# A decoder layer on one core: the output projection taken by halves, the experts' lists in pairs, row additions that skip unrouted places, and half of each expert's second product in split parts

## The chip, the cores and the metric

The kernel runs on one core of a Trainium2 chip. The metric is the device time of one execution in microseconds, the median of several runs. All data is float32.

## The reference, cut to what matters

```python
for i in range(DEPTH):                      # DEPTH = 1, SEQ = 512 tokens, D_MODEL = 1024
    ...                                     # S5 branch and windowed attention give `merged`
    x = x + merged @ w_out[i]               # 512x1024 @ 1024x1024
    h2 = rmsnorm(x, norm_ffn[i])
    x = x + hierarchical_moe(h2, ...)

def hierarchical_moe(h, w_coarse, w_fine, w_up, w_down):
    coarse = softmax(t @ w_coarse)          # 4 groups, the best one is taken
    fine = (t @ w_fine)                     # 16 experts, the best 2 in that group
    ...
    act = silu(g_part) * u_part * gates     # w_up: 1024 -> 2 x 256 for each expert
    out = einsum('nef,efd->nd', act, w_down)  # w_down: 256 -> 1024
```

So 512 tokens with two experts each make 1024 (token, expert) pairs, over 16 experts.

## The kernel before, in words

A float32 product on TensorE costs several passes. The kernel therefore splits most operands into a high and a low part of type fp32r (ScalarE copies the high part, VectorE or GpSimd subtracts it from the raw value), and takes three products of the parts (`product`). The experts' second product and the router take plain float32.

The output projection (`P_OUT`, `NOUT` = 4 weight pieces of 256 columns) goes over `TT` = 4 tiles of 128 tokens. Tile 0 goes piece by piece, the other three take two pieces (512 columns) at once. `x2` is the residual stream. For each tile `norm2` multiplies x2 by the gain into `xg`, ScalarE squares x2 to get the variance, GpSimd takes the inverse root, TensorE transposes xg (`turn_norm2`), VectorE copies it out (`norm2_turned`), `router` multiplies it with the router's weights. These steps of tile t-1 stand between the products of tile t, those of the last tile behind everything.

Then VectorE works out the routing (some 40 small dependent instructions). A list of 128 places is made for each expert: `pos` gives each token a place, first the tokens that are routed to the expert, then the others in order; `pick` compares it with the place numbers, and four matmuls (`place_list`) with `tg` (columns: token number, the gate's high and low part, the token number again) give `idx_all` and `gate_all`. Unrouted tokens have gate 0. The lists of experts 0 to 7 are made before the first expert, those of 8 to 15 at once in step 3.

Step e of the expert loop, in the order of each engine's own queue:

- TensorE: `up(e)` (24 matmuls of 512 columns), in step 3 the lists, `turn_act(e-1)` (2 transposes), `turn_rows(e+1)` (8 transposes), `down_(e-1)` (4 float32 matmuls of 512 columns).
- ScalarE: `high_up(e+1,0)`, `rows_out(e-2)` (PSUM times gate into `y_out`), `high_up(e+1,1)`, `turned_act(e-1)`, a tanh, `high_rows(e+1)`. It waits for the load of expert e+1 at the head of this queue.
- VectorE: in step 3 the lists, `low_up(e+1)` in two halves, `low_rows(e+1)`, `swiglu(e)`.
- GpSimd: `add_rows(e-5)` adds the 128 rows of an expert to the output in memory; it waits until the addition before it has landed. Then it gathers the rows of expert e.
- SyncE loads the weights: 2 MB for `up` into a ring of five places, 1 MB for `down` into four. The first four ring places are those of the output projection's pieces, free when `piece_used` says so; the fifth is x2's. Later, `up` of expert e+5 waits for up(e), and behind it the `down` of e+4 waits for down(e), both in the one queue.

Of the kernel before, what the change touches and what calls it, by code (L numbers as in the profile page):

```python
# [6 lines left out]
F32 = mybir.dt.float32  # L7
# [7 lines left out]
P = 128  # L15
# [9 lines left out]
def hybrid_layer(nc, x, norm_mix, w_in, lam_re, lam_im, log_dt, b_re, b_im, c_re, c_im, d_skip,  # L25
# [26 lines left out]
    LISTS = [0, 2, NE // 2, NE]  # L52
# [7 lines left out]
    with ExitStack() as ctx:  # L60
# [98 lines left out]
        xgT = [part("raw", 2 * D + D * i, D, k=DC, n=P) for i in range(2)]  # L159

# [4 lines left out]
        actT = [part("att", 1280 + 2 * D + 256 * i, 256, k=2, n=P) for i in range(2)]  # L165
        th_e = [part("ssm", 4 * DOWN + 256 * i, 256) for i in range(2)]
# [22 lines left out]
        ssq = sb("ssq", [P, 2 * TT])  # L189
# [25 lines left out]
        idx_all = sb("idx_all", [P, NE], U32)  # L215
        gate_all = sb("gate_all", [P, NE])
# [63 lines left out]
        gather_turn = sem("gather_turn")  # L280

# [58 lines left out]
        def piece_used(eng, n):  # L340
# [35 lines left out]
        def split_low(eng, n):  # L376
# [5 lines left out]
                              ).then_inc(low_done_p if n in on_pool else low_done_v, 1)  # L382

# [30 lines left out]
        def _(sp):  # L414
# [29 lines left out]
            sp.dma_start(sink[:], sinks[0:1, :].broadcast_to([P, HEADS])).then_inc(small_loaded, 16)  # L444
            sp.dma_start(rw[:, :, 0:NG], w_coarse[0].rearrange("(k p) n -> p k n", p=P)).then_inc(small_loaded, 16)
# [54 lines left out]
        def _(g):  # L500
# [137 lines left out]
        def _(act):  # L638
# [169 lines left out]
            for t in range(TT):  # L808
                act.wait_ge(x2_done, NOUT * (t + 1))
                act.activation(part("att", t % 2 * D, D), x2[:, t, :], ACT.Square, accum_out=ssq[:, TT + t:TT + t + 1]).then_inc(sq_done, 1)  # L810
# [3 lines left out]
                act.wait_ge(n2_done, t + 1)  # L814
# [21 lines left out]
            def turned_act(e):  # L836

                act.wait_ge(at_full, e + 1)
                act.activation(actT[e % 2], sc[1][:, 0:2 * P].rearrange("p (k n) -> p k n", k=2), ACT.Copy).then_inc(at_done, 1)  # L839
# [35 lines left out]
            rows_out(NE - 2)  # L875
            turned_act(NE - 1)
# [19 lines left out]
        def _(v):  # L896
# [19 lines left out]
            def norm2(t):  # L916

                if t == 0:
# [3 lines left out]
                if t >= 2:  # L922

                    v.wait_ge(h2_scaled, t - 1)
                    v.wait_ge(tp_full, n_tp + 2 * (t - 1))
                v.wait_ge(x2_done, NOUT * (t + 1))
                tt(xg[t % 2], x2[:, t, :], ffn_gain, ALU.mult).then_inc(n2_done, 1)
                v.wait_ge(sq_done, TT + t + 1)
                mean_var(ssq[:, TT + t:TT + t + 1], D)

            def norm2_turned(t):
                if t >= 2:
                    v.wait_ge(lg_full, t - 1)
                for f in range(2):
                    v.wait_ge(tp_full, n_tp + 2 * t + f + 1)
                    v.tensor_copy(xgT[t % 2][:, 4 * f:4 * f + 4, :], tp[f][:].rearrange("p (k n) -> p k n", k=4)
                                  ).then_inc(h2T_done, 1)
# [63 lines left out]
            v.wait_ge(small_loaded, 16 * 14)  # L1001
# [271 lines left out]

            v.wait_ge(gates_done, 2 * DC)
# [17 lines left out]
            for t in range(TT):  # L1292
                if t:
                    norm2(t - 1)
                for p_ in range(NOUT):
                    n = NOUT * t + p_
                    if t == 0 and p_ + 1 < NOUT:
                        split_low(v, P_OUT + p_ + 1)
                    xs = x2[:, t, p_ * 256:(p_ + 1) * 256]
                    if t == 0:  # L1300
                        v.wait_ge(pj_full, n_pj + n + 1)
                        got = pj[n % 2][:, 0:256]
                    else:
                        v.wait_ge(pj_full, n_pj + NOUT * t + p_ // 2 * 2 + 2)
                        got = pj[p_ // 2][:, (1 - p_ % 2) * 256:(2 - p_ % 2) * 256]
                    stt(xs, got, 0.5, xs, ALU.mult, ALU.add).then_inc(x2_done, 1)
                    if t and p_ == NOUT // 2 - 1:
                        norm2_turned(t - 1)
            norm2(TT - 1)
            norm2_turned(TT - 1)  # L1310

            v.wait_ge(const_ready, 10)
            for n in (0, 3):
                mark(v.tensor_copy(tg[:, :, :, n], bc(tok_id[:, :].rearrange("p (o t) -> p o t", o=1), [P, NE, TT])))
            mark(v.memset(rt[:, 7, 0:1, :], 0.0))
            v.wait_ge(lg_full, TT)
# [53 lines left out]
            v.wait_ge(lg_full, TT + 1)  # L1370
            link(v.tensor_copy(r(10), sc[0][:, 0:TT * NE].rearrange("p (t e) -> p t e", t=TT)))
            mark(ts(r(7), r(6), -1.0, 1.0, ALU.mult, ALU.add))
            v.wait_ge(lg_full, TT + 2)
# [8 lines left out]

# [489 lines left out]
```

## Time and profile before

| | us |
|---|---|
| runs, median (lowest, highest) | 625.59 (621.91, 627.24) |
| the profiled execution's own time | 628.41 |
| its span in the trace | 626.7 |
| mean granted TensorE clock, share of full | 0.931 |
| TensorE busy | 551.8 |
| VectorE busy | 375.3 |
| ScalarE busy | 262.8 |

A busy TensorE is one with a matmul in flight; matmuls overlap, so a row's duration is longer than the step from one start to the next. The chain of waits is the chain of work that ended last, followed back from the last instruction.

### The profile page before, as it was taken

The numbers are of one execution on the slowest core, as the hardware profiler recorded it, in microseconds if no ns is written. First come the engines' busy times: TensorE is split into PE (matmuls) and PEld (weight loads), VectorE is DVE, ScalarE is ACT, GpSimd is POOL, SyncE is SP. The second block draws the span as 40 slices with busy tenths as digits, with TensorE's granted clock in tenths as the row PEclk, the third lists the DMA queues.
The fourth block names the chain that finished last, engine by engine and source line by source line (L and its number), as shares of the span: only waits on it lengthen the run. The fifth ranks groups of instructions, "written<-read, shape, count | busy, mean of one in ns | idle before, by whom it ended". The sixth has DMA issues, their size and how long they took to land.

```text
span 626.7 us, 7175 instructions
## 1 busy us (share of the span) xinstructions
PE 551.8 (88%) x2589; PEld 432.6 (69%) x2589; DVE 375.3 (60%) x615; ACT 262.8 (42%) x421; POOL 191.5 (31%) x354
## 2 busy tenths in 40 slices
PE   1699799999979899989999789935799999999982
PEld 1488687887667677677888678835668677676750
DVE  3885176683983884956666632365865766665530
ACT  6415035435433545364223311131463666665631
POOL 2549333089469269000000000002021341313111
PEclk9999799988989989999999889965897999999997
DMA  8524520220220210113364561597479799999954
GB/s 302 107 69 110 160 66 2 68 67 2 68 67 2 67 51 1 52 51 100 98 208 158 208 253 68 200 396 276 126 262 347 243 376 340 372 341 371 345 96 69
DMA packets 69220, 102.82 MB, mean 164 GB/s; under 512 B 10528, under 2 KB 42304, under 8 KB 69184
## 3 DMA queue, kind: packets, MB, share of 16 engines
q1 hardware_dynamic: 63184, 80.84, 37.6%
q0 software_dynamic: 4608, 16.78, 10.7%
q10 hardware_dynamic: 1392, 4.74, 1.9%
q8 instruction: 21, 0.34, 0.2%
q14 instruction: 15, 0.12, 0.1%
HBM read 88.71 MB, written 12.58 MB: 162 GB/s over the span
## 4 chain that ended last, share of the span: by engine, by line
PE 61%; DVE 15%; DMA 7%; ACT 7%; POOL 4%; issue 3%; SPq 1%; ACTq 0%; POOLq 0%; DVEq 0%
PE pj L1477 8%; PE pj L1479 8%; PE pj L1478 8%; PE m L1794 7%; DMA arena_front<-in_w_expert_up_dram 4%; PE pj L1774 4%; PE pj L1775 4%; PE pj L1776 4%; PE sc L1554 2%; PE tp L1762 2%; ACT arena_back L755 1%; SPq L481 1%; DMA arena_front<-h_rows,idx_all 1%; DVE arena_back L1190 1%; ACT arena_back L764 1%
## 5 line engine op out<-in xcount | busy, mean ns | idle before, releaser
L1477 PE MATMUL pj<-h_high,split 128*128 128x512 f32 x192 | 81.3, 424 | 2.7 <-DVE h_low L963 1.5
L1478 PE MATMUL pj<-h_low,split 128*128 128x512 f32 x192 | 78.4, 409 | 0.0
L1479 PE MATMUL pj<-h_high,split 128*128 128x512 f32 x192 | 78.2, 407 | 0.0
L1411 DVE TENSOR_TENSOR up_low<-arena_front,up_high 128x2048 fp32r<-128x2048 f32 x26 | 59.2, 2290 | 21.9 <-ACT up_high L827 21.9
L1794 PE MATMUL m<-arena_back 128*128 128x512 f32 x128 | 58.3, 598 | 2.8 <-ACT arena_back L839 2.8
L605 POOL DMA_INDIRECT out_dram<-arena_back,idx_all x16 | 29.8, 1866 | 101.2 <-DMA out_dram<-arena_back,idx_all 87.4
L1774 PE MATMUL pj<-up_high,xt_high 128*128 128x512 f32 x128 | 56.1, 438 | 5.3 <-DVE up_low L1411 3.7
L519 POOL TENSOR_TENSOR rstd<-ssq,half_col 128x1 f32<-128x1 f32 x8 | 6.4, 796 | 166.2 <-DVE ssq L940 166.2
L827 ACT ACTIVATE up_high<-arena_front 128x2048 fp32r<-128x2048 f32 x26 | 49.5, 1916 | 6.6 <-DMA arena_front<-in_w_expert_up_dram 5.7
L1775 PE MATMUL pj<-up_low,xt_high 128*128 128x512 f32 x128 | 50.7, 396 | 0.0
L1776 PE MATMUL pj<-up_high,xt_low 128*128 128x512 f32 x128 | 50.7, 396 | 0.0
L1477 PEld LDWEIGHTS pj<-h_high,split 128*128 128x128 f32 x192 | 38.7, 202 | 15.6 <-issue 6.0
L381 POOL TENSOR_TENSOR split<-arena_front,split 128x2048 fp32r<-128x2048 f32 x8 | 36.4, 4551 | 41.3 <-ACT split L374 40.7
L374 ACT ACTIVATE split<-arena_front 128x2048 fp32r<-128x2048 f32 (+1 forms) x23 | 40.4, 1760 | 16.0 <-PE sc L1479 10.0
L1479 PEld LDWEIGHTS pj<-h_high,split 128*128 128x128 f32 x192 | 38.2, 199 | 8.7
L1478 PEld LDWEIGHTS pj<-h_low,split 128*128 128x128 f32 x192 | 38.7, 201 | 7.6
L1794 PEld LDWEIGHTS m<-arena_back 128*128 128x128 f32 x128 | 23.3, 192 | 26.8 <-issue 23.2
L596 POOL DMA_INDIRECT arena_front<-h_rows,idx_all x16 | 18.4, 1151 | 62.1 <-PE tp L1762 40.1
L1477 PE MATMUL pj<-split,m_high 128*128 128x512 f32 (+1 forms) x80 | 30.0, 375 | 6.6 <-DVE split L381 2.8
L381 DVE TENSOR_TENSOR split<-arena_front,split 128x1536 fp32r<-128x1536 f32 (+1 forms) x15 | 30.1, 2004 | 9.6 <-ACT split L374 8.6
L1774 PEld LDWEIGHTS pj<-up_high,xt_high 128*128 128x128 f32 x128 | 24.6, 192 | 14.6 <-issue 6.9
L1406 DVE TENSOR_TENSOR xt_low<-tp,xt_high 128x512 fp32r<-128x512 f32 x32 | 20.7, 685 | 21.7 <-ACT xt_high L833 21.7
(316 smaller groups left out, 1241.4 us busy)
## 6 DMA issues: line engine op xcount, KB each, us to landing
arena_front<-in_w_expert_up_dram SPq DMA_DIRECT2D x13, 2048.0 KB, 15.9
arena_back<-in_w_expert_down_dram SPq DMA_DIRECT2D x16, 1024.0 KB, 12.8
arena_front<-in_w_in_dram SPq DMA_DIRECT2D x13, 1024.0 KB, 5.6
arena_back<-in_w_expert_up_dram SPq DMA_DIRECT2D x3, 2048.0 KB, 17.3
arena_front<-in_w_out_dram SPq DMA_DIRECT2D x4, 1024.0 KB, 5.3
arena_back<-in_x_dram SPq DMA_DIRECT2D x4, 512.0 KB, 5.9
arena_front<-in_w_ssm_glu_gate_dram SPq DMA_DIRECT2D x8, 256.0 KB, 2.8
arena_front<-in_w_ssm_glu_val_dram SPq DMA_DIRECT2D x8, 256.0 KB, 3.6
```

What stands on the lines that cost most here:

```text
L374: nc.scalar.activation(w_high[split_place(n)][:, 0:z], raw[n % 2][:, 0:z], ACT.Copy).then_inc(high_done, 1)
L381: eng.tensor_tensor(w_low[s][:, 0:z], raw[n % 2][:, 0:z], w_high[s][:, 0:z].bitcast(F32), ALU.subtract).then_inc(low_done_p if n in on_poo ...
L605: g.indirect_dma_start(out_rows, bass.IndirectOffsetOnAxis(idx_all[:, e:e + 1], 0), y_out[e % 2], None, compute_op=ALU.add).then_inc(y_add ...
L827: act.activation(up_high[e % 2][:, half(h)], ring[e % NU][:, half(h)], ACT.Copy).then_inc(up_high_done, 1)
L1411: tt(up_low[e % NU][:, half(h)], ring[e % NU][:, half(h)], up_high[e % 2][:, half(h)].bitcast(F32), ALU.subtract).then_inc(up_low_done, 1)
L1477: pe.matmul(dst, sh, mh, start=first and i == 0, stop=False)
L1478: pe.matmul(dst, sh, ml, start=False, stop=False)
L1479: ins = pe.matmul(dst, sl, mh, start=False, stop=last and i == len(terms) - 1)
L1774: pe.matmul(pj[e % 2][:], xs[0], ws[0], start=k == 0, stop=False)
L1775: pe.matmul(pj[e % 2][:], xs[0], ws[1], start=False, stop=False)
L1776: ins = pe.matmul(pj[e % 2][:], xs[1], ws[0], start=False, stop=k == DC - 1)
L1794: ins = pe.matmul(mb[h][:], actT[e % 2][:, k, :], down[e % 4][:, k, h * 512:(h + 1) * 512], start=k == 0, stop=k == 1)
```

## The change

1. The output projection goes over 8 units, `UNITS`: first the left 512 columns of all four tiles, then the right ones. Units 0 and 7 go by pieces of 256 columns, the others in one. In the middle of each unit's products stand the 4 transposes of the unit before, and behind them its half of the router (4 of the 8 terms). TensorE now transposes x2 itself, and the gain is multiplied into the router's weights `rw` once, early; a load `gain_col` (1024 numbers, one each to a partition and column) is added to SyncE's queue at the start. The squares are summed by halves. `piece_used` lets pieces 0 and 1 go after unit 3.
2. The lists of experts 8 to 15 are made in pairs, in steps 1 to 4, and read a step later.
3. `tg`'s fourth column gets token number + 512 for unrouted tokens. It is read into `idx_own`, which the additions use with a bounds check, so that a place with an unrouted token is passed over. The gathers still fetch all 128 rows.
4. The first of the two k-parts of each expert's second product goes in split parts: `high_down` (ScalarE, 128x1024), `low_down` (VectorE, 128x1024), `turned_act` as two copies of 128 columns, `low_act` (VectorE, 128x128); TensorE has two float32 matmuls and six in fp32r where it had four in float32.

```diff
-    LISTS = [0, 2, NE // 2, NE]
+    LISTS = [0, 2] + list(range(NE // 2, NE + 1, 2))
@@ piece_used
-                eng.wait_ge(pj_full, n_pj + NOUT * (TT - 1) + (n - P_OUT) // 2 * 2 + 2)
+                eng.wait_ge(pj_full, n_pj + 2 * TT * ((n - P_OUT) // 2 + 1))
+        UNITS = [(hf, t) for hf in range(2) for t in range(TT)]
+        BY_PIECE = (0, len(UNITS) - 1)
+        LAST_LISTS = len(LISTS) - 3
@@ sync
+            sp.dma_start(gain_col[:], norm_ffn[0].rearrange("(k p) -> p k", p=P)).then_inc(small_loaded, 16)
@@ gpsimd
-                g.indirect_dma_start(out_rows, bass.IndirectOffsetOnAxis(idx_all[:, e:e + 1], 0), y_out[e % 2], None,
-                                     compute_op=ALU.add).then_inc(y_added, 16)
+                g.indirect_dma_start(out_rows, bass.IndirectOffsetOnAxis(idx_own[:, e:e + 1], 0), y_out[e % 2], None,
+                                     compute_op=ALU.add, bounds_check=SEQ - 1, oob_is_err=False).then_inc(y_added, 16)
@@ scalar
+                act.activation(actT[e % 2][:, 1, :], sc[1][:, P:2 * P], ACT.Copy).then_inc(at_done, 1)
+                act.activation(at_high[e % 2][:], sc[1][:, 0:P], ACT.Copy).then_inc(at_done, 1)
+            def high_down(e):
+                act.wait_ge(down_loaded[e % 4], 16 * (e // 4 + 1))
+                act.activation(dn_high[:], down[e % 4][:, 0, :], ACT.Copy).then_inc(dn_high_done, 1)
@@ step(e): behind rows_out(e - 2)
+                if e >= 1:
+                    high_down(e - 1)
@@ vector, output projection
+            for u in range(2, 2 * TT - 1):
+                hf, t = UNITS[u]
+                if hf:
+                    gained(0, t)
+                for i in range(2):
+                    row_piece(u, i)
+                if hf:
+                    gained(1, t)
+                    variance2(t)
+                turned2(u)
+            gained(0, TT - 1)
+            last = 2 * TT - 1
+            row_piece(last, 0)
+            turned2_piece(last, 0)
+            row_piece(last, 1)
+            gained(1, TT - 1)
+            turned2_piece(last, 1)
+            variance2(TT - 1)
@@ vector, expert loop
             for e in range(NE):
-                if e == 3:
-                    fill_lists(2)
+                if 1 <= e <= LAST_LISTS:
+                    for n in range(LISTS[e + 1], LISTS[e + 2]):
+                        pick_list(n)
+                if 2 <= e <= LAST_LISTS + 1:
+                    read_lists(e)
                 if e + 1 < NE:
                     low_up(e + 1, 0)
+                if e:
+                    low_down(e - 1)
+                if e + 1 < NE:
                     low_up(e + 1, 1)
+                if e:
+                    low_act(e - 1)
+                if e + 1 < NE:
                     low_rows(e + 1)
                 swiglu(e)
@@ tensor, output projection
+            for u in range(1, 2 * TT - 1):
+                ...
+                out_pair(u, first_k)
+                for i in range(2):
+                    turn_rows2(u - 1, i)
+                out_pair(u, last_k).then_inc(pj_full, 2)
+                router(u - 1)
+            ...
+            out_piece(u, 0, first_k)
+            for i in range(2):
+                turn_rows2(u - 1, i)
+            out_piece(u, 0, last_k).then_inc(pj_full, 1)
+            router(u - 1)
+            out_piece(u, 1, first_k)
+            turn_rows2(u, 0)
+            out_piece(u, 1, last_k).then_inc(pj_full, 1)
+            turn_rows2(u, 1)
+            router(u)
@@ down_(e)
                 for h in range(2):
-                    for k in range(2):
-                        ins = pe.matmul(mb[h][:], actT[e % 2][:, k, :], down[e % 4][:, k, h * 512:(h + 1) * 512], start=k == 0, stop=k == 1)
+                    pe.matmul(mb[h][:], actT[e % 2][:, 1, :], down[e % 4][:, 1, cols[h]], start=True, stop=False)
+                pe.wait_ge(dn_low_done, e + 1)
+                pe.wait_ge(at_low_done, e + 1)
+                for h in range(2):
+                    pe.matmul(mb[h][:], at_high[e % 2][:], dn_high[:, cols[h]], start=False, stop=False)
+                    pe.matmul(mb[h][:], at_high[e % 2][:], dn_low[e % 4][:, cols[h]], start=False, stop=False)
+                    ins = pe.matmul(mb[h][:], at_low[e % 2][:], dn_high[:, cols[h]], start=False, stop=True)
                 ins.then_inc(dn_full, 1)
```

## Rows read from the trace of the kernel before

**Rows 1.** Windows: us, busy time (instructions) of each engine, granted clock, DMA share, GB/s

```profile
360.30:362.20 1.90, 0.00 (x0) 0.00 (x0) 1.90 (x2) 0.00 (x0) 0.00 (x0) 1.00 1.03 414
362.20:367.60 5.40, 5.33 (x28) 5.23 (x29) 0.86 (x3) 0.23 (x1) 0.00 (x0) 0.68 0.99 392
488.80:594.40 105.60, 105.60 (x445) 75.15 (x446) 67.77 (x63) 66.40 (x83) 29.22 (x19) 1.00 1.04 350
```

**Rows 2.** Chain of waits (start, us, what), output projection to first gather

```profile
378.67 1.69 PE sc L1701 x16
...
385.97 0.87 PE tp L1695 x8
...
405.98 0.77 DVE arena_back L1306 x2
406.87 1.24 DVE arena_front L927
...
410.25 3.42 PE sc L1701 x16
413.69 0.69 DVE arena_back L1319 x4
...
428.02 7.14 DMA arena_front<-h_rows,idx_all
```

**Rows 3.** DMA issues in the window 435:448: form, count, median us to landing

```profile
arena_front<-h_rows,idx_all POOLq DMA_INDIRECT x1, 4.4
```

**Rows 4.** Timeline of TensorE (start, us, line, operation): lists, a middle expert

```profile
476.39 0.95 PE L1753 MATMUL sc<-tg,pick 128*128 128x4 f32 x8
...
543.61 0.39 PE L1774 MATMUL pj<-up_high,xt_high 128*128 128x512 f32 x1
...
544.29 0.38 PE L1784 MATMUL sc<-ident,arena_back 128*128 128x128 f32 x2
```

**Rows 5.** Chain of waits, second products of four steps

```profile
467.63 3.44 PE m L1794 x8
...
484.99 3.80 PE m L1794 x8
...
525.51 3.44 PE m L1794 x8
535.53 3.44 PE m L1794 x8
```

**Rows 6.** Timeline of VectorE, a middle step (idle before it in brackets)

```profile
552.18 2.29 DVE L1411 TENSOR_TENSOR up_low<-arena_front,up_high 128x2048 fp32r<-128x2048 f32 x1 [1.72 <-ACT up_high L827]
```

**Rows 7.** Timeline of ScalarE, the same step

```profile
554.73 0.38 ACT L839 ACTIVATE arena_back<-sc 128x256 f32<-128x256 f32 x1 [2.58 <-PE sc L1784]
```

**Rows 8.** Timeline of SyncE's queue: loads for the experts' first products

```profile
399.64 10.31 SPq L467 DMA_DIRECT2D arena_front<-in_w_expert_up_dram  x4
...
448.38 0.37 SPq L467 DMA_DIRECT2D arena_front<-in_w_expert_up_dram  x1
...
489.23 0.47 SPq L467 DMA_DIRECT2D arena_front<-in_w_expert_up_dram  x1
```

**Rows 9.** Chain of waits, the last load and the end

```profile
566.51 24.80 DMA arena_front<-in_w_expert_up_dram
...
596.53 3.70 PE m L1794 x8
...
610.21 1.27 ACT arena_back L848 x2
...
611.75 6.26 DMA out_dram<-arena_back,idx_all
```

**Rows 10.** Timeline of GpSimd, two additions

```profile
544.46 1.59 POOL L605 DMA_INDIRECT out_dram<-arena_back,idx_all  x1 [7.28 <-DMA out_dram<-arena_back,idx_all]
...
618.76 1.55 POOL L605 DMA_INDIRECT out_dram<-arena_back,idx_all  x1 [5.46 <-DMA out_dram<-arena_back,idx_all]
```

**Rows 11.** DMA queues in the window 611.5:626.7: packets, MB, share of 16 engines

```profile
q0 software_dynamic: 288, 1.05, 44.8%
```

More of the change, by code:

```diff
@@ L159, in hybrid_layer @@
         xgT = [part("raw", 2 * D + D * i, D, k=DC, n=P) for i in range(2)]
+        x2T = [part("rot", 512 * i, 512, k=4, n=P) for i in range(2)]
         xt_high = [rounded("xt_high0", "raw", 2 * D, [P, DC, P]), rounded("xt_high1", "u4", 0, [P, DC, P])]
@@ L165, in hybrid_layer @@
         actT = [part("att", 1280 + 2 * D + 256 * i, 256, k=2, n=P) for i in range(2)]
+        at_high = [rounded(f"at_high{i}", "att", 1280 + 2 * D + 256 * i, [P, P]) for i in range(2)]
+        at_low = [rounded(f"at_low{i}", "att", 1792 + 2 * D + P * i, [P, P]) for i in range(2)]
+        dn_high = rounded("dn_high", "att", 0, [P, D])
+        dn_low = [rounded(f"dn_low{s}", "ssm", s * DOWN, [P, D]) for s in range(4)]
         th_e = [part("ssm", 4 * DOWN + 256 * i, 256) for i in range(2)]
@@ L280, in hybrid_layer @@
         gather_turn = sem("gather_turn")
+        dn_high_done, dn_low_done, at_low_done = (sem(n) for n in ("dn_high_done", "dn_low_done", "at_low_done"))
         pj_order, tp_order = [], []
@@ L875, in _ @@
             rows_out(NE - 2)
+            high_down(NE - 1)
             turned_act(NE - 1)
@@ L1419, in swiglu, with low_down, low_act @@
                 stt(act_e[b], a1_e[b], 0.5, pj[b][:, DE:UP_N], ALU.mult, ALU.mult).then_inc(act_done, 1)
+            def low_down(e):
+                v.wait_ge(dn_high_done, e + 1)
+                tt(dn_low[e % 4][:], down[e % 4][:, 0, :], dn_high[:].bitcast(F32), ALU.subtract).then_inc(dn_low_done, 1)
+            def low_act(e):
+                v.wait_ge(at_done, 2 * (e + 1))
+                tt(at_low[e % 2][:], sc[1][:, 0:P], at_high[e % 2][:].bitcast(F32), ALU.subtract).then_inc(at_low_done, 1)
             low_rows(0)
@@ L1732, in _, with turn_rows2 @@
-            turn_norm2(TT - 1)
-            router(TT - 1)
+            def turn_rows2(u, i):
+                hf, t = UNITS[u]
+                pe.wait_ge(x2_done, 2 * u + i + 1)
+                if u < 2:
+                    pe.wait_ge(tp_free[u], (n_tp + 1 - u) // 2)
+                else:
+                    pe.wait_ge(h2T_done, 2 * u if u == BY_PIECE[1] and i else 2 * (u - 1))
+                for k in range(2):
+                    c0 = hf * 512 + (2 * i + k) * P
+                    ins = pe.transpose(turned_bank(u, i)[:, k * P:(k + 1) * P], x2[:, t, c0:c0 + P], ident[:])
+                ins.then_inc(tp_full, 1)
@@ new lines, in router, with out_piece @@
+            def router(u):
+                hf, t = UNITS[u]
+                for k in range(4):
+                    if k % 2 == 0:
+                        pe.wait_ge(h2T_done, 2 * u + k // 2 + 1)
+                    ins = pe.matmul(sc[0][:, t * (NG + NE):(t + 1) * (NG + NE)], x2T[u % 2][:, k, :], rw[:, 4 * hf + k, :],
+                                    start=u == 0 and k == 0, stop=hf == 1 and k == 3, skip_group_check=True)
+                ins.then_inc(lg_full, 1)
+            def out_piece(u, i, ks):
+                hf, t = UNITS[u]
+                w = piece_w(P_OUT + 2 * hf + i, k=DC, n=256)
+                tok = slice(t * P, (t + 1) * P)
+                for k in ks:
+                    if u == 0 and i == 0:
+                        pe.wait_ge(m_low_done, k + 1)
+                    ins = product(out_bank(u, i), [(both(m_hl, k, tok), both(w, k, slice(None)))], k == 0, k == DC - 1)
+                return ins
@@ new lines, in out_pair @@
+            def out_pair(u, ks):
+                hf, t = UNITS[u]
+                tok = slice(t * P, (t + 1) * P)
+                w2 = [x[:, hf].rearrange("p s (k n) -> p s k n", k=DC) for x in (out_high, out_low)]
+                return product(pj[(u + 1) % 2][:].rearrange("p (s n) -> p s n", s=2),
+                               [(both(m_hl, k, tok), both(w2, slice(None), k, slice(None))) for k in ks], ks[0] == 0, ks[-1] == DC - 1)
+            first_k, last_k = range(DC // 2), range(DC // 2, DC)
@@ L1735, in _ @@
+            u = 2 * TT - 1
+            pe.wait_ge(x2_done, 2 * (u - 1))
+            out_piece(u, 0, first_k)
+            for i in range(2):
+                turn_rows2(u - 1, i)
[6 more added lines that the diff above has]
+            router(u)
             pe.wait_ge(r_pe, 1)
```

198 lines of the change are left out of this document (96 added, 102 removed).

## The prediction

> **What bounds the kernel now.** I read the windows first. From 488.8 to 594.4 us TensorE is busy without a gap at the full clock, and the DMA share is 1.04: both are full, and a change that helps one of them alone soon meets the other [rows 1]. In the output projection there is a hole of 1.9 us and behind it 5.4 us at a mean clock of 0.68 [rows 1]. The chain of waits says where the path runs: TensorE to 405.98, then a serial stretch of VectorE, transposes, a router at 3.42 us instead of 1.69, the routing, and the first gather (7.14 us, landed at 435.2) [rows 2]. At the end it leaves TensorE: it passes through a weight load of 24.8 us (issued at 566.51, landed at 591.31), two second products, an addition to memory and the last addition [rows 9]. TensorE's own steps are 525.51 to 535.53, 10.02 us each [rows 5]; 535.53 to 596.53 is 61.0 us for six steps, 0.9 more than six times 10.02, so the late load costs about 0.9 us now [rows 5, 9].
>
> **Output projection.** Matmuls are the same: 96 of 256 columns, 144 of 512. The hole at 360.3 (1.9 us) is tile 0 waiting for the fourth weight piece [rows 1]. By halves the pieces 2 and 3 are wanted only at unit 4, behind three units of some 6.8 us, so the hole goes, and with it the slow clock behind it: 0.32 of 5.4 us, 1.7 us [rows 1]. Together 3.6. The earlier stalls (fp32r parts of m, piece 1) stay. Against it, more transposes and router work now stand ahead of the last product: before it were 3 x 0.87 and 2 x 1.69 = 6.0 us [rows 2]; after it are 7.5 halves of the transposes (3.3) and 7 halves of the router (5.9), 9.2 us. The last product ends 0.4 us earlier.
>
> Behind it stood 405.98 to 413.69, 7.7 us: additions, gain product 1.24, transposes, copies, router 3.42 [rows 2]. Now: addition of one piece 0.4 (half of 0.77), two transposes 0.3, a gain product of half width 0.6, a copy 0.4, four of the router's instructions 0.4 to 0.9, and 0.1 for each handover, 2.6 to 3.0 us. The variance (a square of half width, VectorE, GpSimd's root) runs beside it and should end at about the same time. That saves 4.9. In the routing itself `tg`'s new column adds one dependent instruction and two small copies, 0.4 us by the sizes around it (0.69 for four) [rows 2]. So the first gather is asked for 4.9 us earlier.
>
> Two of the four first loads go at about 377 instead of 399.64 [rows 8], when the DMA has little to do. They are 4 MB of the 10 MB that stood ahead of and beside the first gather. That gather took 7.14 us from its issue, one with the queue free 4.4 [rows 2, 3]: between 0 and 2.7 saved; I take 2.7, since the last of the loads should now be down by 422. The loads themselves gain nothing more: all five places were full before up(0) ended anyway, and load 5 waits for it. Sum up to up(0): 7.6 us earlier. The added load and the scaling of `rw` stand in stretches where VectorE waits for other loads; by the sizes of their neighbours 0 to 0.5 us if that cover is gone, 0 taken.
>
> **Lists.** From 467.63 to 484.99 one step takes 17.36 us, and its second product 3.80 for 3.44: 7.7 us over a plain one [rows 5]. TensorE and VectorE take turns there, and the clock falls. In pairs, VectorE makes both `pick`s before TensorE needs them, and TensorE pays 8 matmuls, 0.95 us [rows 4], in four steps: 3.8. Saved 3.9. If the picks aren't hidden, two of 0.69 more in each step; the cover is VectorE's idle time, about 3.6 us a step (105.6 us hold 67.8 busy, ten and a half steps) [rows 1].
>
> **Second product.** Eight float32 records take 3.44 us, 0.86 for a matmul of 512 columns [rows 5]; three fp32r products take 544.29 - 543.61 = 0.68 [rows 4]. Two of four are exchanged: 2 x 0.18 = 0.36 us for each expert, 5.4 over the 15 ahead of the last. This is the time on TensorE; the rest must be hidden. ScalarE gets 1.2 us more (1.27 for two of 512 columns [rows 9]) and 0.2 for a second copy, of an idle 2.58 [rows 7]. VectorE gets 1.24 (as the gain product [rows 2]) and 0.3; before, it ended low_up at 552.18 + 2.29 = 554.47, with 1.72 idle ahead of it, and up ended at 544.29 + 10.02 = 554.31 [rows 4, 6]. Following the queues, in a step of 9.65 us low_act is done about 1.4 us after up ends, and TensorE wants it at 2.8 (transposes 1.1, two float32 products 1.7): covered by 1.4, and by 0.9 in the steps with lists. So 0 for that; next would be low_act.
>
> TensorE alone would thus come to 7.6 + 3.9 + 5.4 + 0.9 (the late load gone) = 17.8 us earlier at its last second product.
>
> **The loads.** This is the step on which the size depends. A faster TensorE asks for loads sooner, but the DMA was full from the load issued at 489.23 to the landing at 591.31: 102.1 us [rows 1, 8, 9]. That load came 40.85 us after the one behind up(0) [rows 8]. Now it comes 40.85 - 7.7 + 3 x 0.95 - 3 x 0.36 = 34.9 us after. If the work of the queue is the same, the last weights land 137.0 us after up(0) instead of 142.9: with the 7.6 us, 13.5 us earlier than before, against some 17 that TensorE could use. ScalarE waits for this load at the head of its queue, with high_down now behind it as well (1.1 later), and two cheaper second products give back 0.7. The second product of the last expert would come 13.1 us earlier.
>
> Does the passing over relieve the queue? Of 2048 places 1024 are routed, so half of the rows go. An addition with the queue free takes 44.8% of 15.2 us / 2 = 3.4 us of all 16 engines [rows 11], so the most that it can give is 1.7 for each of the 12 additions in the full stretch, 20 us, far more than the 4 that are missing. The least is nothing. The reason for nothing is in how the rows are dealt out: the two additions have 288 packets, 2 x (128 + 16), so every one of 16 engines has eight rows and one packet more [rows 11]. Routed tokens stand first in the list; an addition and a load are done when their slowest engine is. If an engine's rows are a block of places, the engines of the first half of the list keep all eight, and only the others are relieved. If the rows are dealt in turn, all are relieved. No row of before decides it. I take no relief, because the packets show a fixed share to each engine, and keep the other end for the range.
>
> The Trainium skill, page "DMA: Bandwidth & Descriptors", section "The descriptor swizzle", says that a 128-partition transfer is dealt by partition, engines 0 to 7 serving partitions 0 to 63. By that rule about the first 64 places keep their engines as busy as before and the additions become no shorter: the first of the two results below. No row here shows which engine took which row.
>
> **The sum.** Without relief the last two additions are as before: 611.75 + 6.26, then 618.76 to the end [rows 9, 10]. -13.1 against the profiled 628.41 (its span is 626.7, 1.7 less) gives 615.3; the median of the runs lies 2.8 below that execution, so 612.5. I say 612.
>
> **Rivals.**
> *The additions relieve all engines.* For it: half of the rows are gone; against it the fixed shares. Then TensorE is the bound to the end, -17.8. The end itself shortens: each of the last two additions takes 1.7 us less, half of the 3.4 [rows 11]; but the last second product comes about 1 us later behind high_down, so that the last addition finds its rows ready only 0.6 us sooner: -2.3. Together -20.1, median 605.5.
> *The new work isn't covered.* VectorE's chain (low_up, low_down, low_up, low_act) is longer than I followed it and TensorE waits in each step. It decides from 1.4 us a step. At 0.4 us over that, 15 x 0.4 = 6 takes the gain of the split away; with the loads then just in time, median 613 to 621, say 617.
> *The check makes the additions slow to issue.* An issue takes 1.59 us, and an addition starts when the one before has landed, every 10.0 us in the middle (7.28 of that waiting) [rows 10]. With two result buffers rows_out, and with it TensorE, waits once this chain falls about 5 us further behind. If going through 128 indices with a check costs 2 us more each time, the chain goes at 12.0: 15 x 2.0 - 5 = 25 us later than the steps of 10.0, beside 12 earlier at the front: median about 638. It decides from about 1.3 us more per issue. Against it: 1.59 us for 128 rows is 12 ns for a row, and a comparison is little beside building the row's descriptor.
> *The change doesn't pass over anything* (all rows still go): the same as the forecast.
>
> **How the numbers follow.** Forecast (no relief, or none in effect) 0.47, with its own range 607 to 617: 2.7 for the gather, 2 for the end of the loads to either side. Full relief 0.32 (601 to 608). New work not covered 0.13. Slow additions 0.06; other 0.02. About 1%, 6.3 us, is what a measurement of this kernel can tell from no change; faster by more is below 619.3. Forecast and relief lie below it wholly, of the third case two thirds: 0.47 + 0.32 + 0.08 = 0.87; within 1% 0.07; slower 0.06. The range 601 to 618 leaves out most of the last two cases' far sides.
>
> **What would show it.** The hole at 360 is gone and the router's last part ends near 408; the first gather starts near 423 and takes under 5 us; steps 1 to 4 take 10.6 us each, later ones 9.65, with second products of 3.1; the lists' step of 17 us is gone. The forecast is right if the DMA share stays at 1.04 from 480 on, the last load takes over 25 us to land and TensorE waits 3 to 5 us in the last steps, and if an addition at the end still takes 6.3 us. The relief shows in a share below 1 in the middle and an addition of about 4. I am wrong if low_act or dn_low ends TensorE's waits in the middle, or if GpSimd's issues grow beyond 3 us.

## The result, and the profile after

The changed kernel takes 620.83 us, the median of 20 runs (616.33 to 625.73), against 626.04 for 20 runs of the kernel before (621.91 to 632.18). The ratio is 0.9909, with a 95% interval of 0.9887 to 0.9932, so some 4 to 7 us faster. 612 was predicted, with a range of 601 to 618. Its profiled execution took 618.26 us (span 616.5, mean clock 0.944).

The two profiled executions differ by 10.2 us, more than the medians do. Not all of that belongs to the change: the first matmul of the projection's second weight piece, which lies ahead of all that the change reorders, starts at 353.00 us before and at 350.06 after. It stands anywhere from 347.5 to 355.0 in kernels that are the same up to there. So 2.9 us of the 10.2 are scatter, and I compare the traces from fixed places on. From that first matmul to the end of the span it is 273.7 us before and 266.4 after, 7.3 less. From the first row of the routing (413.69 before [rows 2], 405.27 after) to the end it is 213.0 and 211.2, only 1.8 less. The experiments differ behind the routing only, and are compared from its first row too.

The chain of waits of the kernel after (start, us, what):

```profile
398.98 0.80 PE sc L1806 x8
...
405.27 0.69 DVE arena_back L1390 x4
...
419.97 7.84 DMA arena_front<-h_rows,idx_all
...
472.65 1.72 PE m L1916 x4
...
483.17 1.72 PE m L1916 x4
...
501.61 0.87 PE tp L1883 x8
...
511.23 0.87 PE tp L1883 x8
...
555.17 24.35 DMA arena_front<-in_w_expert_up_dram
579.57 1.80 issue
581.36 1.25 ACT arena_back L890 x2
582.61 0.95 ACT dn_high L881
583.55 1.81 ACT up_high L863
...
601.58 3.31 PE m L1916 x4
...
609.07 1.25 POOL out_dram L636
```

The front end did what it should: the routing starts 8.4 us earlier than in [rows 2]. The steps with lists take 10.52 us (472.65 to 483.17), the later ones 9.62 to 9.64 (501.61 to 511.23), where it was 17.36 and 10.02 [rows 5]. But the gather takes 7.84 us where 4.4 was counted on (7.14 before; in the experiments that leave its surroundings as they are it takes 7.2 to 8.1). At the end the chain runs through the last load as it did [rows 9], and behind it dn_high now stands ahead of up_high.

Windows of the same kernel (us, busy time of PE, PEld, DVE, ACT, POOL, granted clock, DMA share, GB/s):

```profile
362.20:367.60 5.40, 5.40 (x31) 4.51 (x29) 2.18 (x3) 0.00 (x0) 0.00 (x0) 1.00 0.42 167
...
390.00:404.00 14.00, 13.48 (x99) 12.44 (x97) 6.02 (x12) 3.59 (x6) 0.83 (x2) 1.00 0.39 154
404.00:419.10 15.10, 4.18 (x21) 3.81 (x20) 11.55 (x58) 5.33 (x7) 0.55 (x1) 0.62 0.97 349
419.10:427.80 8.70, 5.47 (x24) 5.34 (x24) 4.42 (x11) 0.00 (x0) 2.81 (x2) 0.50 0.97 349
...
500.00:560.00 60.00, 59.60 (x274) 45.77 (x273) 46.56 (x47) 43.33 (x61) 19.30 (x12) 1.00 0.98 342
544.30:579.50 35.20, 31.69 (x141) 23.34 (x140) 23.60 (x24) 22.17 (x30) 10.62 (x7) 1.00 0.96 325
579.50:606.70 27.20, 22.78 (x85) 15.08 (x83) 11.63 (x14) 12.87 (x21) 6.33 (x3) 0.94 0.30 57
```

The stretch that had a granted clock of 0.68 [rows 1] has 1.00. While the gather is under way the DMA share is 0.97. In the last two stretches TensorE is idle for 3.5 and 4.4 us. Most of that is time behind late loads; the last two waits, 0.37 and 2.31 us, are not, since e1 below has both of them although its loads are in time. ScalarE waits for the loads at the head of its queue (waits from 340 us on: us, times, longest):

```profile
POOL out_dram L636 <- DMA out_dram<-arena_back,idx_own: 91.6, 14, 8.6
...
ACT up_high L863 <- DMA arena_front<-in_w_expert_up_dram: 12.6, 4, 4.4
```

SyncE's queue: the first four loads go in two pairs; then the fifth, the one behind up(0), and the last of these loads:

```profile
374.18 0.99 SPq L498 DMA_DIRECT2D arena_front<-in_w_expert_up_dram  x2
...
402.98 0.99 SPq L498 DMA_DIRECT2D arena_front<-in_w_expert_up_dram  x2
416.57 0.37 SPq L498 DMA_DIRECT2D arena_back<-in_w_expert_up_dram  x1
...
441.49 0.37 SPq L498 DMA_DIRECT2D arena_front<-in_w_expert_up_dram  x1
...
555.17 4.25 SPq L498 DMA_DIRECT2D arena_front<-in_w_expert_up_dram  x1
```

And TensorE's timeline at the last expert's second product:

```profile
601.58 3.31 PE L1916 MATMUL m<-arena_back 128*128 128x512 f32 x4 [2.31 <-ACT arena_back L875]
603.90 1.42 PE L1920 MATMUL m<-dn_high,at_high 128*128 128x512 f32 x1
```

The last addition alone (window 608.5 to 616.5). The first line is the busy share of the 16 DMA engines in 40 equal slices, in tenths; then packets, MB, share of 16 engines, and its issue with us to landing:

```profile
DMA  0000000000019047023635636556200000000000
...
q0 software_dynamic: 144, 0.27, 23.4%
...
out_dram<-arena_back,idx_own POOLq DMA_INDIRECT x1, 6.2
```

GpSimd's timeline gives what it waited for:

```profile
608.77 1.55 POOL L636 DMA_INDIRECT out_dram<-arena_back,idx_own  x1 [5.87 <-ACT arena_back L890]
```

It moves about half of the bytes (65 of 128 rows) and keeps the engines busy for 23.4% of 8.0 us = 1.87 us, where 44.8% of 15.2 / 2 = 3.4 us were used [rows 11]. It lands in 6.2 us nevertheless; the last but one of before took 6.26 [rows 9].

### The profile page after: what moved, and what is told of

It is laid out like the page before. It is cut to its first block, busy times and chain, and to the rows that moved or that the text cites. A ratio compares the mean times of both kernels' runs of the same rounds, so it can differ in the third digit from the quotient of the medians.

```text
span 616.5 us, 7391 instructions
## 1 busy us (share of the span) xinstructions
PE 540.5 (88%) x2621; PEld 431.0 (70%) x2621; DVE 400.0 (65%) x665; ACT 279.2 (45%) x461; POOL 196.6 (32%) x354
## 4 chain that ended last, share of the span: by engine, by line
PE 58%; DVE 15%; DMA 10%; ACT 8%; POOL 4%; issue 3%; SPq 1%; ACTq 0%; POOLq 0%; DVEq 0%
PE pj L1578 9%; PE pj L1580 8%; PE pj L1579 8%; DMA arena_front<-in_w_expert_up_dram 8%; PE pj L1895 3%; PE m L1916 3%; PE pj L1896 3%; PE pj L1897 3%; PE sc L1655 2%; PE tp L1883 1%; DMA arena_front<-h_rows,idx_all 1%; ACT arena_back L786 1%; DVE arena_back L1253 1%; ACT arena_back L795 1%; DVE up_low L1493 1%
## 5 line engine op out<-in xcount | busy, mean ns | idle before, releaser
L636 POOL DMA_INDIRECT out_dram<-arena_back,idx_own x16 | 33.3, 2079 | 101.6 <-DMA out_dram<-arena_back,idx_own 91.6
L1895 PE MATMUL pj<-up_high,xt_high 128*128 128x512 f32 x128 | 51.1, 399 | 5.3 <-DVE up_low L1493 3.7
L1916 PE MATMUL m<-arena_back 128*128 128x512 f32 x64 | 31.9, 624 | 6.1 <-ACT arena_back L875 6.1
L627 POOL DMA_INDIRECT arena_front<-h_rows,idx_all x16 | 20.2, 1260 | 50.1 <-PE tp L1883 32.2
L1580 PE MATMUL pj<-split,m_low 128*128 128x512 f32 (+1 forms) x80 | 28.4, 355 | 0.0
L1897 PEld LDWEIGHTS pj<-up_high,xt_low 128*128 128x128 f32 x128 | 24.6, 192 | 5.4
```

The lines of the kernel that those rows point to most:

```text
L1580: ins = pe.matmul(dst, sl, mh, start=False, stop=last and i == len(terms) - 1)
L1895: pe.matmul(pj[e % 2][:], xs[0], ws[0], start=k == 0, stop=False)
L1897: ins = pe.matmul(pj[e % 2][:], xs[1], ws[0], start=False, stop=k == DC - 1)
L1916: pe.matmul(mb[h][:], actT[e % 2][:, 1, :], down[e % 4][:, 1, cols[h]], start=True, stop=False)
```

## The experiments

Each is the changed kernel with the edit shown. "From the routing" is the span of its profiled execution from the routing's first row to the end: 211.2 us for the changed kernel. Ratios are to the kernel before, timed with each group of experiments on the same chip; from the routing, each figure is one execution.

### What the passing over gives, and to whom

Theory: the additions move half of the bytes, but the DMA engines that serve the first half of the places stay as busy as before, so neither the additions nor the loads beside them end sooner. Rival: the loads are not the bound, and something else eats the gain.

`e1_spread`: the order of the places in `slot_no`, so that each group of four partitions holds either low places or high ones, and partitions 0 to 31 and 64 to 95 have the low ones.

```diff
-            g.iota(slot_no[:], pattern=[[1, CAP]], ...
+            g.iota(slot_no[:], pattern=[[8, 2], [64, 2], [1, 8], [16, 4]], ...
```

> The changed kernel with the place numbers of a list permuted, so that routed tokens (the first ones in the list) are laid over all 16 engines if the engine is 8 x (place / 64) + (place / 4 mod 8). Theory A (the additions relieve only the engines that hold the second half of the places): now all engines are relieved, the last addition falls from 6.2 us to about 4.5, the load that landed at 579.5 comes 5 us or more earlier, TensorE's waits in the last four steps (about 1 to 2 us each) go, and the time falls by 6 to 10 us. Theory B (a row that is passed over costs as much as one that is moved, or the flight is latency): no change, within 1 us. Theory C (the late load only uncovers the new order of the queues; the load itself is late for lack of total DMA time): the share is the same on average, so at most 2 us.

Measured: 611.12 us, ratio 0.9756 (0.9704 to 0.9807); 202.5 from the routing, 8.7 less. The waits of ScalarE for loads are gone, and all but one of GpSimd's for landed additions too (from 400 us on):

```profile
POOL out_dram L636 <- ACT arena_back L890: 72.4, 15, 8.1
...
POOL out_dram L636 <- DMA out_dram<-arena_back,idx_own: 4.4, 1, 4.4
```

Its last addition alone (window 602.6 to 609.6) lands in 5.2 us, where about 4.5 was expected:

```profile
DMA  0000000000000990261199958311000000000000
...
q0 software_dynamic: 144, 0.27, 31.3%
...
out_dram<-arena_back,idx_own POOLq DMA_INDIRECT x1, 5.2
```

`e2_block`: another order, in which each block of eight partitions has four low places and four high ones.

```diff
+            g.iota(slot_no[:], pattern=[[1, 16], [16, 8]], ...
```

> The same idea for the other way of dealing: places permuted so that routed tokens are laid over all engines if the engine is place / 8. 
Measured: 620.05 us, ratio 0.9895 (0.9834 to 0.9955), 211.6 from the routing: as the changed kernel. So the order doesn't help by being mixed; it has to be mixed in the right way. Its last addition (window 613 to 621.7) lands in 6.3 us:

```profile
DMA  0000000000000924903076452654210000000000
```

`e3_noskip`: the additions take `idx_all` without a bounds check, as before.

> The changed kernel with all 128 rows of each list added (the list with true token numbers for all places, no bounds check), the rest as changed. Theory A: the engines of the first places are as busy as in the changed kernel, so the time is the same within 1.5 us. If the passing over does relieve the loads already: slower by 3 us or more, with the last loads landing later.

Measured: 620.68 us, ratio 0.9904 (0.9873 to 0.9936). As placed in the change, passing over unrouted rows is worth nothing that the runs can tell (213.3 from the routing, 2.1 more, in one execution each).

`e12_spread_noskip`: the order of e1, and the additions of e3.

> Spread places, but the additions pass over nothing: every one of 128 rows is added, as in the kernel before. If the gain of the spread places (1.5% of the time before) comes from the passing over being dealt evenly to the 16 engines, it goes here: the ratio returns to that of the changed kernel, 0.990, with the last addition at 6.2 us. If the order of the places helps by itself (gathers and additions touching other rows at a time), it stays at 0.976.

Measured: 619.41 us, ratio 0.9892 (0.9843 to 0.994), 210.8 from the routing. The gain of e1 is gone. Its last addition (window 607.5 to 615.5), and its waits (from 400 us on):

```profile
DMA  0000000000099392766899999997200000000000
...
POOL out_dram L636 <- DMA out_dram<-arena_back,idx_all: 96.3, 15, 8.4
```

The four kernels form a square. In the old order passing over leaves the ratio where it was (0.9904 without, 0.9909 with it); in the new one it takes off 0.0136 (0.9892 and 0.9756), 8.5 us. The order brings nothing without the passing over. So the gain is the relief, evenly dealt. The packets show the dealing. Behind the first short peak, which all four have, the busy share of the last addition is at most 0.7 in the changed kernel and in e2; in e1 and e12 it reaches 0.9. Counted from the traces' DMA records, 8 packets of 4 KB are under way at a time for 1.90 us in the changed kernel (never more than 11), in e2 for 1.93 us (never more than 11). In e1 it is 16 for 1.20 us, and 16 for 1.71 us in e12, up to 20 in both. So with rows passed over, about half of the engines do all the work in the changed kernel and in e2, and all of them share it in e1.

The page "DMA: Bandwidth & Descriptors" of the Trainium skill, section "The descriptor swizzle", gives each engine, in a transfer to 128 partitions, two groups of four partitions, 32 apart, engines 0 to 7 the first 64 partitions. By that rule the changed kernel and e2 leave eight engines with all their rows and e1 leaves every engine with about half; the three runs and the counts of packets agree. Which engine took which row is not seen in the traces.

### What the split second product is worth

`e4_nosplit`: four float32 matmuls again, without `high_down`, `low_down`, `low_act`. `e8_spread_nosplit`: the same on top of e1.

```diff
-            high_down(e - 1) ... low_down(e - 1) ... low_act(e - 1)
-                    pe.matmul(mb[h][:], at_high[e % 2][:], dn_high[:, cols[h]], ...)   # and dn_low, at_low
+                    for k in range(2):
+                        ins = pe.matmul(mb[h][:], actT[e % 2][:, k, :], down[e % 4][:, k, cols[h]], ...)
```

> The changed kernel with the experts' second product wholly in float32, as before (no high_down, low_down, low_act). Theory A (the end is set by the loads): the middle steps take 10.0 us instead of 9.64 but the last load lands at nearly the same distance, high_down is not behind it and the last product isn't split: the same time or up to 2 us faster. Rival (TensorE's time counts): slower by 15 x 0.36 = 5.4 us.

> The spread lists with the second product wholly in float32. With the unspread lists this was about 2 us faster than the split one. If the loads were the bound there and TensorE is the bound now, it is slower than the spread lists with the split by 15 x 0.36 = 5.4 us less what the plain end gives back (2 to 2.5): 3 us slower, steps of 10.0 us against 9.64. Rival (the split itself isn't worth anything): the same or faster.

Measured: e4 618.32 us, ratio 0.9886 (0.9837 to 0.9934), 209.1 from the routing; e8 615.69 us, 0.9835 (0.9779 to 0.9892), 206.1. While the loads bind, the split brings nothing and perhaps costs 1 to 2 us (0.9909 against 0.9886, the intervals overlap). Once they don't, it saves 3.6 us from the routing (3 was expected) and 0.0079 of the time, 4.9 us, the intervals overlapping a little; 5.4 were predicted for TensorE. In e4, steps take 10.02 us instead of 9.64, and the last load still lands 173.8 us behind the routing's first row, against 174.3: TensorE's pace did not set it.

### The first gather

`e5_hold`: e1, and the fifth load waits until the first gather has landed. `e11_hold_alone`: the same without e1's order.

```diff
             sp.wait_ge(x2_stored, 16 * TT)
+            sp.wait_ge(gathered[0], 16)
             load_up(4)
```

> The spread lists and one thing more: SyncE asks for the fifth weight load only when the first gather has landed. In the changed kernel that gather took 7.8 us, with the load issued at 416.57 and the gather at 419.97, where a lone gather takes 4.4. If the fifth load is what the gather shares the DMA with, it takes about 4.5 us now and everything behind it comes 3 us earlier (ratio 0.005 lower than with spread lists alone). Rival: the gather is slow for another reason (its rows were stored only shortly before, or the second gather runs beside it), and it stays above 7 us; or the later load is missed in step 3 and costs as much.

> The changed kernel with its own order of places, and the fourth weight load held until the first gather has landed. It tells whether time gained at the first gather reaches the end while the loads bind. If the last weights land at a fixed distance behind the load that follows the first expert's products, the 3 us gained at the gather come through whole: 3 us less from the projection's second piece to the end. If the queue has a fixed amount of work from 489 us on and is simply full, the last load lands when it did, and nothing or at most 1 us is gained.

Measured: e5 608.99 us, ratio 0.9743 (0.969 to 0.9796), 199.8 from the routing, 2.7 less than e1. The ratio is only 0.0013 lower (0.005 was expected), 0.8 us, less than the runs can tell. Its first gather lands in 4.7 us (window 420 to 427, in which a second is issued whose landing the trace lacks):

```profile
arena_front<-h_rows,idx_all POOLq DMA_INDIRECT x2, 4.7
```

up(0) starts 25.4 us behind the routing's first row instead of 28.5. So the fifth load is what stretched the gather (e11's first gather also takes 4.7 us, with the old order of places); what stands next is TensorE, which has 24 matmuls of the second lists ahead of the transposes.

e11: 617.94 us, ratio 0.9852 (0.9796 to 0.9908), 210.3 from the routing, 1.0 less than the changed kernel. Here up(0) is 2.9 us sooner (25.4 instead of 28.3), the load behind it 2.3 (33.9 instead of 36.2), but the last load lands only 0.9 sooner (173.4 instead of 174.3). By this one execution two thirds of a gain at the front are lost in the full queue. The medians (a ratio 0.0057 lower, 3.6 us) allow the whole of it, with overlapping intervals, so this stays open. (The expectations of e11 and e9 call this load the fourth; it is `load_up(4)`, the fifth.)

### Smaller edits

`e7_gather`: e1, and the gathers pass over unrouted places too.

```diff
-                                     bass.IndirectOffsetOnAxis(idx_all[:, e:e + 1], 0)).then_inc(gathered[e % 2], 16)
+                                     bass.IndirectOffsetOnAxis(idx_own[:, e:e + 1], 0),
+                                     bounds_check=SEQ - 1, oob_is_err=False).then_inc(gathered[e % 2], 16)
```

> The spread lists, and the gathers pass over unrouted places too (rows of unrouted places keep what the buffer held; their gate is 0). If the first gather is slow by its own bytes, it falls from 7.8 to 5 to 6 us and the time by 2 us. If it is slow by the loads beside it, by half of that or less. In the middle nothing should change, since with spread lists TensorE no longer waits for loads: within 1 us.

Measured: 609.16 us, ratio 0.974 (0.9691 to 0.979); 201.9 from the routing, 0.6 less than e1, too little to tell. The first gather takes 7.02 us there and 8.08 in e1, where 5 to 6 was expected if its own bytes set it.

`e6_lastplain`: e1, with the last expert's second product in plain float32 and without `high_down(15)`, `low_down(15)`, `low_act(15)`.

> The spread lists, and the last expert's second product in float32 as before (15 of 16 in split parts). In the changed kernel TensorE waited 2.3 us for it behind high_down, and its first four records ran at half the clock (3.31 us instead of 1.98). If that is the cost of the split at the end, the gap is 1.5 us, the product 3.7 us instead of 5.1, and the end comes 2 to 2.5 us earlier. Rival: the last addition waits for the addition before it, so that half or more of this is lost.

Measured: 609.26 us, ratio 0.9732 (0.9684 to 0.9781); 200.8 from the routing, 1.7 less than e1 (2 to 2.5 was expected). TensorE's last second product:

```profile
596.29 3.70 PE L1919 MATMUL m<-arena_back 128*128 128x512 f32 x8 [1.47 <-ACT arena_back L877]
```

It waits 1.47 us instead of 2.31, and its 3.70 us compare with 5.05 (601.58 to 606.63) for the split one of the changed kernel. The granted clock is 1.00 over the 3.70 us and 0.66 over the 5.05.

`e10_order`: the changed kernel with one move in VectorE's queue.

```diff
                 if e:
                     low_down(e - 1)
+                    low_act(e - 1)
                 if e + 1 < NE:
                     low_up(e + 1, 1)
-                if e:
-                    low_act(e - 1)
```

> The changed kernel with one thing changed: on VectorE low_act(e - 1) stands ahead of low_up(e + 1, 1), which waits for ScalarE's copy of a load. Theory: in the last steps, where the loads come late, TensorE's second part of a second product waits for at_low only because low_act is queued behind the low part of a late load; with it ahead, the four waits of TensorE on at_low (1.8 us in all) go, and the time falls by 1 to 2 us. Rival: low_act moved forward waits itself for at_high, up to 3 us in each step, and pushes low_up(e + 1, 1) and so the up products later; then the steps in the middle grow beyond 9.64 us and the time rises by up to 10 us.

Measured: 623.18 us, ratio 0.9924 (0.989 to 0.9958); 215.4 from the routing, 4.1 more. My theory fell: nothing was gained. Of the rival, the longer steps are shown; that the whole becomes slower is not, since the ratio is only 0.0015 above the changed kernel's and the intervals overlap. VectorE's timeline of a middle step:

```profile
507.52 0.29 DVE L1509 TENSOR_TENSOR at_low<-sc,at_high 128x128 fp32r<-128x128 f32 x1 [2.42 <-ACT at_high L876]
507.73 2.28 DVE L1493 TENSOR_TENSOR up_low<-arena_front,up_high 128x2048 fp32r<-128x2048 f32 x1
509.92 1.28 DVE L1488 TENSOR_TENSOR xt_low<-tp,xt_high 128x512 fp32r<-128x512 f32 x2
```

VectorE waits 2.42 us with low_up queued behind it, and TensorE's next first product waits for xt_low. The chain of waits shows up_low every 10.2 us, where a step took 9.6:

```profile
497.58 2.20 DVE up_low L1493
...
507.81 2.19 DVE up_low L1493
...
518.02 2.20 DVE up_low L1493
```

`e9_all`: the edits of e1, e5, e6 and e7 together.

> The version with spread places, the fourth weight load held behind the first gather, the gathers passing over unrouted places, and the last expert's second product in plain float32, all four together. Each of the last three was run on top of the spread places and took 4.1, 0.7 and 3.1 us off the stretch from the projection's second piece to the end in its one profiled execution, but only 0.1 to 0.3% off the ratio of the medians. If the profiled savings are real and add up, this comes 7 to 8 us below the version with spread places alone: ratio to the kernel before 0.963 to 0.966. If they are mostly scatter between executions, it stays at the ratio that each of them had, 0.971 to 0.975.

Measured: 607.48 us, ratio 0.9674 (0.9627 to 0.972), the best of all and faster than both kernels; 198.5 from the routing, 3.9 less than e1. The ratio is 0.0082 lower than e1's, 5.1 us. The 4.1, 0.7 and 3.1 us in the expectation were taken from the projection's second piece and had scatter between it and the routing in them: from the routing they are 2.7, 0.6 and 1.7, together 4.9, so 3.9 to 5.1 is nearly the sum. The ratio itself lies between the two ranges that were expected (0.963 to 0.966 and 0.971 to 0.975), and its interval reaches into both. A window of it, where TensorE has no gap and the queue moves more than in the changed kernel (342 GB/s):

```profile
500.00:560.00 60.00, 60.00 (x275) 46.45 (x275) 49.60 (x50) 47.17 (x62) 17.31 (x13) 1.00 1.05 378
```

## Why the prediction was wrong

The direction was right, and so was the choice that the additions give no relief and the loads set the end; but two steps failed, the first gather and the end behind the last load, and the fall came out at less than half of the forecast (5.2 us between the medians, where the sum had 13.1). The forecast took 13.1 us off the profiled execution. From the projection's second piece on, 7.3 came off. By its steps:

| step | predicted | measured |
|---|---|---|
| routing's first row | -5.3 | -5.5 (60.69 to 55.21 behind the second piece) |
| routing to the gather's issue | +0.4 | +0.4 (14.33 to 14.70) |
| gather and up(0), to the load behind up(0) | -2.7 | +1.2 |
| that load to the landing of the last one | -5.9 | -4.9 (142.9 to 138.0) |
| landing to the end of the last second product | +0.4 | +2.9 (24.2 to 27.1) |
| from there to the end | 0 | -1.3 (11.2 to 9.9) |
| sum (before rounding) | -13.1 | -7.3 |

*Output projection: right.* The hole and the low clock behind it went, the serial stretch became short, and the gather is asked for 5.1 us earlier (4.9 predicted).

*The gather: the step that failed most.* I wrote that the last of the loads "should now be down by 422". I had followed the first four and not the fifth. It waits until the residual rows are stored, and is issued at 416.57 instead of 418.73, 2.2 us earlier, while the gather came 8.0 us forward. (In both, 2.9 are scatter: counted from the second piece, the load comes 0.8 us later and the gather 5.1 sooner.) So it stood 9.3 us ahead of the gather before (428.02 [rows 2]) and 3.4 now, and more of it lies beside the gather. With loads 3 and 4 at 402.98, the DMA sat at 0.39 from 390 to 404 and was full just when the gather came. e5 and e11 take the fifth load away: the gather then lands in 4.7 us, near the 4.4 that were taken. The saving was there, but the change's own order of loads used it up. Its error is 3.4 us: 2.7 predicted and 0.7 lost, the 0.7 being no more than the scatter of 7.2 to 8.1 among like runs. By e11's trace only about a third of it would have reached the end, since the queue is full later; by the medians it may have been all.

*The lists and the split product: right on TensorE, and hidden by the loads.* Steps of 10.52 and 9.62 to 9.64 us, 10.6 and 9.65 predicted; low_act (502.29 in a middle step) ends before TensorE wants it; only from 544 us on, behind late loads, TensorE waits for it four times, 1.8 us in all. The rival of work that isn't covered fell, though narrowly: in e10 one wrong place in VectorE's queue makes a step 0.6 us longer. As predicted, TensorE alone would have come further: e1 has it.

*The loads: the mechanism right, 1.0 off.* 137.0 us from the load behind up(0) to the last landing, 138.0 measured. The assumption beneath it, a fixed distance from that load, isn't safe: in e11 it is 139.4.

*The end behind the last load: the second failed term.* I counted high_down as 1.1 and two cheaper products as -0.7. The chain has dn_high twice: 0.95 us in front of up_high, and once more in front of the last copy of the activations, so that TensorE stands still for 2.31 us instead of 1.47, 0.84 more. And the last split product is no cheaper: 5.05 us instead of 3.70 [rows 9], 1.35 more, where I had 3.1. The granted clock accounts for it: the expert before runs the same product at 1.00 in 3.4 us (595.70 to 599.06), and here, behind the longer wait, it is 0.66. The prediction had no term for it. Less 0.36 for the product of expert 14 that is 2.8; 2.9 were measured. e6 takes the last two terms away and gets 1.7 of their 2.2. On the other side, 1.3 come back: before, the last addition waited until the one ahead of it had landed [rows 10]; now its rows are late enough that it waits for ScalarE only.

*The additions: the forecast's choice was right.* No relief, although half of the bytes went; 6.2 us for the last, as predicted. But one of my signs was wrong: the DMA share did not stay at 1.04, it is 0.98, and yet ScalarE waits for loads. A share below 1 in the middle was my sign for the relief, and by itself it would have misled. The share is a mean over 16 engines, and half-idle engines lower it: between 500 and 560 us the additions land in a median of 9.2 us, 9.3 before, and in 8.0 in e1. The last load took 24.35 us, just short of the "over 25" that I had asked for. The full relief is real when the rows are dealt evenly: 0.9756, some 611 us, 5.5 more than the 605.5 of that rival, about what the gather (8.08 us there) and the last product were off by. The slow issue fell: 1.55 and 1.59 us are the usual values with the bounds check and without [rows 10]. Single issues go beyond my sign of 3 us with it (3.38 at 573.95), but without it too (3.24 at 585.31 in e12).

The rest of the distance from 612 to 620.8 (8.8 us): 5.8 are the table's sums, 2.1 lie between the fall of the medians (5.2) and that of the traces (7.3), and about 0.9 are the median of before, 0.45 higher over 20 runs, and rounding.

## What to carry to other kernels

When work is taken out of a transfer, ask which of the engines it is taken from. Here 8 packets at a time instead of 16 carried the rows that were left, the addition landed no sooner, and a mean share of 0.98 hid it. The order of the places in a list was free here, and spreading the idle ones evenly was worth 1.5%. When a path is moved forward, list every transfer that may now lie beside its first step, and see which of them moved with it and which stayed.

## What was not expected of the hardware

- A passed-over row keeps a packet of a few bytes: 144 packets with 128 rows and with 65 of them, of which 79 instead of 16 are under 512 bytes.
- Alone, an addition takes 6.2 to 6.3 us for 128 rows in either order (44.3% of 8.0 us busy in e12), 6.2 for half of them in the old order, 5.2 when evenly dealt (over the last three additions of all runs that pass over rows it is 5.9 to 6.7 us in the order of the change or of e2, and 4.5 to 5.9 in that of e1). So in an idle queue the even dealing saves only 1 us; in the full one (500 to 560 us) the whole moves 380 GB/s instead of 342.
- The clock at the end. TensorE does nothing for 2.31 us, and the first fp32r product behind the gap takes 1.42 us where the same instruction of the expert before takes 0.79. The granted clock is 0.62 from 601.5 to 603.9 us and 0.71 from 603.9 to 606.7, between the two levels of 1.2 and 2.4 GHz (0.5 and 1.0), so part of each stretch ran at the lower one. In e6, where the gap is 1.47 us, it stays at 1.00 over the whole product. The second stretch of the changed kernel:

```profile
603.90:606.70 2.80, 2.73 (x8) 1.50 (x6) 0.00 (x0) 0.00 (x0) 0.00 (x0) 0.71 0.42 69
```
